# Two transformer blocks in split single precision: residual stream token-major, products 512 columns wide, layers unrolled

## The reference, cut to what matters

```
for l in 2 layers:                                   # block 1
    h = rms_norm(x, ln1)
    proj = h @ w_in                                  # 2866 columns: q, k, v, gates of three mixers
    mixed = [nsa(...), mla(...), retention(...)]     # 17 attention heads of 64 or 96, 5 retention heads
    x = x + mixed @ w_out                            # 1024 x 1024
    h = rms_norm(x, ln2)
    x = x + square(relu(h @ w_up)) @ w_down          # 1024 x 4096, 4096 x 1024
x = rms_norm(x, final_gain)
for l in 2 layers:                                   # block 2
    sh1, sc1, g1, sh2, sc2, g2 = split(silu(c) @ w_ada + b_ada, 6)      # w_ada: 1024 x 6144
    h = rms_norm(x, n1) * (1 + sc1) + sh1
    pool, conv, attention of 8 heads, three gates    # from h @ w_in
    merged = sum of three gated products
    x = x + g1 * (merged @ w_out)
    h = rms_norm(x, n2) * (1 + sc2) + sh2
    x = x + g2 * ((silu(h @ w_gate) * (h @ w_up)) @ w_down)             # 2816 inner features
```

## Time and profile before

| | |
|---|---|
| median of 3 runs | 1811.67 us (1810.47 to 1813.94) |
| the profiled execution: time, span of its trace | 1813.12 us, 1811.3 us |
| PE, DVE, ACT, POOL busy, share of the span | 91%, 63%, 48%, 10% |
| mean granted TensorE clock | 0.907 |
| split products on PE | some 10,400, three for each pair of a weight block and an activation chunk |
| read from memory | 293.67 MB, 163 GB/s over the span |

### The profile page before, as it was taken

How to read it: one execution, slowest core, us unless ns; L and a number is a source line. 1 busy time by engine, 2 the same in 40 slices (tenths; PEclk the granted TensorE clock), 3 DMA queues, 4 the chain that set the end, 5 groups by cost and what they waited for, 6 DMA issues and landing times.

```text
span 1811.3 us, 32196 instructions
## 1 busy us (share of the span) xinstructions
PE 1642.5 (91%) x11986; PEld 1556.2 (86%) x11986; DVE 1142.6 (63%) x1867; ACT 862.2 (48%) x1450; POOL 175.8 (10%) x108
## 2 busy tenths in 40 slices
PE   2998978899799887989979999799997999889999
PEld 2995778899799677979968998799997999879999
DVE  4746868964574686896447755656645864666653
ACT  4443456653443345665337553444444754344442
POOL 0001411300000230230000302100000200300000
PEclk7987589999897658999989999999998999889999
DMA  5432554765343245475523433335553344335552
GB/s 210 164 116 117 185 187 175 299 224 187 111 171 117 104 175 200 183 292 212 184 93 120 183 141 140 139 140 180 179 186 110 140 149 157 138 111 178 180 186 92
DMA packets 41344, 296.89 MB, mean 164 GB/s; under 512 B 4576, under 2 KB 4576, under 8 KB 5600
## 3 DMA queue, kind: packets, MB, share of 16 engines
q1 hardware_dynamic: 40752, 293.57, 44.9%
q10 hardware_dynamic: 432, 1.17, 0.2%
HBM read 293.67 MB, written 1.05 MB: 163 GB/s over the span
## 4 chain that ended last, share of the span: by engine, by line
PE 73%; DVE 13%; issue 7%; ACT 4%; POOL 1%; DMA 1%; DVEq 0%; ACTq 0%; POOLq 0%; SPq 0%
PE acc L708 20%; PE acc L709 20%; PE acc L710 20%; DVE wL L1398 3%; DVE ring L1385 1%; PE acc L852 1%; PE ps_s L784 1%; PE acc L763 1%; PE ps_t L791 1%; PE ps_s L783 1%; ACT wH L1131 1%; DVE hL L1407 1%; PE acc L768 1%; DMA nv<-pos 1%; PE acc L933 1%
## 5 line engine op out<-in xcount | busy, mean ns | idle before, releaser
L708 PE MATMUL acc<-hH,wH 128*128 128x256 f32 x2368 | 700.2, 296 | 91.8 <-DVE hL L1407 72.2
L1398 DVE TENSOR_TENSOR wL<-ring,wH 128x1024 fp32r<-128x1024 f32 x444 | 546.7, 1241 | 300.7 <-ACT wH L1131 299.8
L709 PE MATMUL acc<-hL,wH 128*128 128x256 f32 x2368 | 681.1, 288 | 0.0
L710 PE MATMUL acc<-hH,wL 128*128 128x256 f32 x2368 | 680.5, 287 | 0.0
L1131 ACT ACTIVATE wH<-ring 128x1024 fp32r<-128x1024 f32 x444 | 464.2, 1050 | 229.7 <-PE acc L710 213.4
L708 PEld LDWEIGHTS acc<-hH,wH 128*128 128x128 f32 x2368 | 464.1, 196 | 113.2 <-DVE hL L1407 83.8
L709 PEld LDWEIGHTS acc<-hL,wH 128*128 128x128 f32 x2368 | 466.6, 197 | 2.4 <-issue 1.9
L710 PEld LDWEIGHTS acc<-hH,wL 128*128 128x128 f32 x2368 | 465.8, 197 | 0.0
L708 PE MATMUL acc<-aH,wH 128*128 128x256 f32 x864 | 244.5, 283 | 0.0
L709 PE MATMUL acc<-aL,wH 128*128 128x256 f32 x864 | 244.5, 283 | 0.0
L710 PE MATMUL acc<-aH,wL 128*128 128x256 f32 x864 | 244.5, 283 | 0.0
(11 more groups left out here) (278 smaller groups left out, 2006.1 us busy)
## 6 DMA issues: line engine op xcount, KB each, us to landing
ring<-stream SPq DMA_DIRECT2D x276, 1024.0 KB, 4.8
cst<-consts SPq DMA_DIRECT2D x1, 1669.0 KB, 10.8
x<-xin SPq DMA_DIRECT2D x1, 1024.0 KB, 5.7
out<-x SPq DMA_DIRECT2D x4, 256.0 KB, 4.4
onc<-once ACTq DMA_DIRECT2D x1, 516.0 KB, 10.6
v1all<-vec ACTq DMA_DIRECT2D x1, 371.0 KB, 5.9
v2all<-vec SPq DMA_DIRECT2D x1, 330.0 KB, 11.5
nv<-pos ACTq DMA_DIRECT2D x1, 256.0 KB, 11.7
```

The costliest lines, as they stand in the source:

```text
L708: pe.matmul(out, w[0], y[0], start=first, stop=False)
L709: pe.matmul(out, w[0], y[1], start=False, stop=False)
L710: return pe.matmul(out, w[1], y[0], start=False, stop=last)
L1398: TTN(wL[:, u % SPLIT, :], ring[:, t % RING, half * UNIT:(half + 1) * UNIT], wH[:, u % SPLIT, :].bitcast(F32), ALU.subtract).then_inc(lo_r ...
```

## The change

- `x` is token-major: 2 x 128 tokens on the partitions, 1024 features along the free axis. It is transposed in at the start and out at the end, on PE.
- The down, out (`wo`), value (`v`) and token-major (`tm`) products take the activations as the stationary operand and 512 weight columns as the moving one (`wide_units`, `wo_unit`): for a unit 12 products of 512 columns in place of 24 of 256. Two banks, one for each half of the tokens, are filled together.
- A wide unit takes 128 columns of weights from each of four half tiles. The ring has eight slots of half a tile. Groups of four halves lie in four aligned slots (`align`); `gathered` and `placed` view them for the split.
- Norms: the sum of squares comes from ACT's square with a sum along the free axis (`square`), the root is taken of 128 x 2 elements, DVE scales x into `z` (`normalize`), PE transposes z, ACT makes the high part with the gain (`gained`, `shifted_h`), DVE the low part (`lows`). The first two units after a norm are computed together (`project_both`).
- The gates g1 and g2 of block 2 and the final gain are needed along the free axis now: `diagonals` and two products with ones for each half make rows of them.
- Modulation is computed on DVE alone, a half tile after a unit. No tile of it lies in attention: 2 are among the projections, 10 in up, 12 in down.
- In up, ACT does relu, square and the copy to aH; DVE only the low part.
- The rotary angles are computed after the first four units are fed. The feed of the first four out units stands at step 6 of attention. In block 2 the first out units are interleaved with the mix (`MIX_ORDER`).
- The four hardware loops are gone: the layers are written out.

```diff
-RING = 4
+SLOTS = 8
...
+class Stream:
+    def half(self, kind, j, h, align=1):
+        t = self.tiles.index((kind, j))
+        self.load((kind, j, h), [(t, h * UNIT, UNIT, 0)], align)
+        return (kind, j, h)
+    def unit(self, keys, part, n, name):
+        self.units.append((keys, part, n, name))
+        if self.waiting:
+            self.ada_after[len(self.units) - 1] = [self.waiting.pop(0)]
+    def ada(self, j):
+        for h in range(2):
+            self.waiting.append(self.half("ada", j, h))
+    def wide(self, keys, n, parts, names):
+        for q in range(parts):
+            self.unit(keys, q, n, names[q])
...
+def stream1():
...
+    for u in range(F1 // 2):
+        s.plain("up", u, 0, f"up{2 * u}")
+        s.plain("up", u, 1, f"up{2 * u + 1}")
+        if u % 3 != 2 and u < 15:
+            s.ada(j)
+            j += 1
+    for h in range(2):
+        names = unit_names("dn", h, F1 // 2) + [f"dn{h}1"]
+        for g in range(4):
+            kh, hh = g // 2, g % 2
+            keys = [s.half("down", 2 * n + kh, hh, 4 if n % 4 == 0 else 1) for n in range(4 * h, 4 * h + 4)]
+            s.wide(keys, P, 4, names[4 * g:4 * g + 4])
+            for _ in range(2):
+                if j < N_ADA:
+                    s.ada(j)
+                    j += 1
...
+MIX_ORDER = ["A0", "A1", "A2", "A3", "wo0.0", "A4", "A5", "wo0.1", "A6", "A7", "wo0.2", "wo0.t1"]
...
+def lay_out():
+    loads, at, seq = [], {}, 0
+    latest, landed = [None] * SLOTS, [0] * SLOTS
+    for i, (_, s, _, base) in enumerate(LAYER_LIST):
+        for key, pieces, align in s.loads:
+            seq += -seq % align
+            slot = seq % SLOTS
+            seq += 1
...
+            def wait_free(load):
+                turns, _, L, _ = LAYER_LIST[load.layer]
+                kind, j, h = load.key
+                if kind == "ada":
+                    sp.wait_ge(ada_dve, L * (2 * N_ADA) + 2 * j + h + 1)
+                elif kind in WHOLE_USER:
+                    sp.wait_ge(acc_full, turns.full(WHOLE_USER[kind], L))
+                else:
+                    sp.wait_ge(lo_ready, load.last_unit + 1)
...
+            for load in ALL_LOADS[SLOTS:]:
+                if load.before is not None:
+                    wait_free(load.before)
+                fetch(load)
...
+            def wide_units(names, units, y, n, between=None):
+                outs = [open_acc(name) for name in names]
+                for k in range(units):
+                    wh, wl = [v.rearrange("p (c n) -> p c n", n=512) for v in next_unit()]
+                    for t in range(TT):
+                        for c in range(2):
+                            hh, hl = y(2 * k + c, t)
+                            last = split_product(outs[t][:, 0:n], (hh, hl), (wh[:, c, 0:n], wl[:, c, 0:n]),
+                                                 k == 0 and c == 0, k == units - 1 and c == 1)
+                        if k == units - 1 or t == TT - 1:
+                            last.then_inc(acc_full, 1)
...
             def feed(count):
-                tn, L = fed["tn"], fed["L"]
...
+                    if not unit.part:
+                        for load in unit.loads:
+                            act.wait_ge(got[load.slot], load.landed)
                     if u >= SPLIT:
+                        act.wait_ge(acc_full, ALL_UNITS[u - SPLIT].release)
+                    act.activation(placed(wH, unit, u), gathered(ring, unit), ACT.Copy).then_inc(hi_ready, 1)
...
-                    act.activation(aH[:, n, :], r4[n % 4], ACT.Square).then_inc(aH_ready, 1)
+                    act.activation(tmp4[n % 4], r4[n % 4], ACT.Square).then_inc(up_squared, 1)
+                    act.wait_ge(up_squared, L * F1 + (n + 1))
+                    act.activation(aH[:, n, :], tmp4[n % 4], ACT.Copy).then_inc(aH_ready, 1)
...
+            def feed(count):
+                for u in range(fed["next"], min(fed["base"] + count, len(ALL_UNITS))):
+                    unit = ALL_UNITS[u]
+                    dve.wait_ge(hi_ready, u + 1)
+                    TTN(placed(wL, unit, u), gathered(ring, unit), placed(wH, unit, u).bitcast(F32), ALU.subtract)\
+                        .then_inc(lo_ready, 1)
+                    fed["next"] = u + 1
+                    for key in LAYER_LIST[unit.layer][1].ada_after.get(unit.local, ()):
+                        ada(unit.layer, key)
...
+            def normalize(k, dst=None, row=None):
+                dve.wait_ge(ss_ready, 4 * (k + 1))
+                link(TTN(stat[:, 2, :], sums[:, 0, :], sums[:, 1, :], ALU.add))
+                TSC(stat[:, 0, :], stat[:, 2, :], 1.0 / D, EPS, ALU.mult, ALU.add).then_inc(var_ready, 1)
+                dve.wait_ge(y_ready, roots(k))
+                link(TTN(stat[:, 2, :], stat[:, 1, :], stat[:, 1, :], ALU.mult))
+                link(STT(stat[:, 2, :], stat[:, 0, :], -0.5, stat[:, 2, :], ALU.mult, ALU.mult))
+                link(STT(stat[:, 3, :], stat[:, 2, :], 1.5, stat[:, 1, :], ALU.add, ALU.mult))
+                for h in range(2):
+                    for t in range(TT):
+                        at = slice(512 * h, 512 * h + 512)
+                        if row is None:
+                            TSC(z[:, t, at], x[:, t, at], stat[:, 3, t:t + 1], None, ALU.mult).then_inc(z_ready, 1)
...
-                TTN(products, products, cb2, ALU.mult).then_inc(ada_pool, 1)
```

More of the change, by code:

```diff
@@ L113, in split_units, with __init__, load, plain @@
[L113 to L120 removed]
+class Stream:
+    def __init__(self, tiles):
+        self.tiles = tiles
+        self.loads, self.units, self.ada_after = [], [], {}
+        self.waiting = []
+    def load(self, key, pieces, align=1):
+        self.loads.append((key, pieces, align))
+    def half(self, kind, j, h, align=1):
[6 more added lines that the diff above has]
+            self.ada_after[len(self.units) - 1] = [self.waiting.pop(0)]
+    def plain(self, kind, j, h, name):
+        self.unit([self.half(kind, j, h)], None, None, name)
+    def whole(self, kind):
+        for h in range(2):
+            self.half(kind, 0, h, 2 if h == 0 else 1)
+    def ada(self, j):
[4 more added lines that the diff above has]
+            self.unit(keys, q, n, names[q])
+    def end(self):
+        self.ada_after.setdefault(len(self.units) - 1, []).extend(self.waiting)
+        self.waiting = []
+        return self
@@ new lines, in by_columns, with out_half, blocks_at @@
+def by_columns(s, kind, js, names):
+    for h in range(2):
+        keys = [s.half(kind, j, h, 2 if j == js[0] else 1) for j in js]
+        s.wide(keys, 256, 2, names[2 * h:2 * h + 2])
+def out_half(s, h):
+    return [s.half("wout", n // 2, n % 2, 4 if n % 4 == 0 else 1) for n in range(4 * h, 4 * h + 4)]
+def blocks_at(m, count):
+    first = min(count, 16 - m % 16)
+    out = [(m // 16, (m % 16) * P, first * P, 0)]
+    return out + ([(m // 16 + 1, 0, (count - first) * P, first * P)] if first < count else [])
@@ L641, in rest @@
-            def rest(tiles, turns, units, lo_base, layer, first):
-                for t in range(RING, len(tiles)):
-                    wait_free(tiles, turns, units, lo_base, layer, t - RING)
-                    load(t % RING, first + t)
-            def ahead(tiles, turns, units, lo_base, layer, first):
-                n = len(tiles)
-                for t in range(n - RING, n):
-                    wait_free(tiles, turns, units, lo_base, layer, t)
-                    load(t % RING, first + n + t % RING)
@@ L1028, in _, with mix @@
                 pe.wait_ge(yc_ready, L * 2 + 2)
[L1029 removed]
+                def mix(n):
                     wh, wl = blocks(next_unit())
@@ L1119, in feed, with square @@
-            def feed(count):
-                tn, L = fed["tn"], fed["L"]
-                for u in range(fed["next"], min(count, len(fed["units"]))):
-                    t, half, _ = fed["units"][u]
-                    slot = t % RING
-                    if half == 0:
-                        n = len([v for v in range(len(fed["tiles"])) if v % RING == slot])
-                        act.wait_ge(got[slot], L * (16 * n) + 16 * (fed["visits"][slot] + t // RING + 1))
+            def square(junk, h, t):
+                act.activation(junk[:, 2 * h + t, :], x[:, t, 512 * h:512 * h + 512], ACT.Square,
+                               accum_out=sums[:, h, t:t + 1]).then_inc(ss_ready, 1)
@@ L1285, in _ @@
                     feed(units_before(i + 1) + SPLIT)
+                    if i in ROWS_AT:
+                        for g in range(2):
+                            take(A2, f"row{ROWS_AT[i]}{g}", L, rows[ROWS_AT[i]][:, 512 * g:512 * g + 512], n=512)
                     if i in SQUARES_AT:
@@ L1777, in _ @@
+            normalize(2 * LAYERS, row=gain_row)
+            end_layer()
+            for L in range(LAYERS):
+                fed["base"] = UNIT_BASE[LAYERS + L]
                 nc.vector.memset(up_[:, :, 0:16], 0.0)
```

1009 lines of the change are left out of this document (586 added, 423 removed).

## The result

The changed kernel took 1911.99 us (median of 4 runs, 1908.34 to 1916.78), the one before 1812.12 beside it: 1.055 times as long, 95% interval 1.052 to 1.058. I had forecast 1792, range 1745 to 1828, and slower with a chance of 0.20. What I took for a small gain is a loss of 100 us.

A forecast was written before the change was run, and what follows sets the result against it. The prediction took TensorE's (PE's) stream to set the end, with 73% of the chain. Gains of 129 us less losses of 110 took the span from 1811.3 to a forecast of 1792 us, range 1745 to 1828.

The forecast's parts named there:

- The ring stall: In down of block 1, weight groups and modulation halves leave no second buffer, so PE stops: 103 us lost in all.
- Up: Modulation on VectorE alone, without slow DVE instructions beside POOL's, saves 9.5 us a layer in up, 19 us.
- The first product: At the start, first product near 22 us instead of 40.05, fifth near 45.5 instead of 55.5; 8.5 us gained.
- Layer to layer in block 1: Boundary after down of block 1: PE's wait falls from 13 us to about 7.8, a gain of 4.6.
- the landing term of the ring: In down of block 1, five half tiles land 8.3 us after release, making a group's cycle 18.9 us.
- Rival C: Ring cycle longer than 21 us, through dearer strided feeds or a queue behind SP: 1816 to 1835 us, chance 0.10.
- the mix: In block 2, out units between mix products partly fill PE's idle time: 2.5 us a layer, 5 gained.
- Block 2's projections: Projection segment of block 2 grows by 2.2 us over both layers.
- Wide products: Products of 512 columns take 0.216 us, replacing two of 256 at 0.240 together; 51 us gained with token-major.
- Boundaries: Shorter waits around norms gain 29.5 us, including final norm 9, out to up 0.5 twice, block 2 layer to layer 7.3.
- attention: Block 1's attention loses its 14 modulation tiles a layer: 8 us a layer, 16 gained, between 4 and 13.
- the likeliest case: Ring stall against the other gains, ending at 1760 to 1808 us; chance 0.66.

The follow-up runs named there:

- run 2: Changed kernel without the 12 modulation tiles in down of block 1 (loads, product and sum left out, half of the modulation zero): 1777.80 us, 0.983 times before.
- run 12: Changed kernel, groups and layout kept, all modulation computed but moved out of down of block 1 into up and the projections: 1843.38 us, 1.020 times before.
- run 1: Changed kernel with block 1's down weights in memory as used, one wide unit in one half tile: 1843.61 us, 1.019 times before.
- run 7: Changed kernel with its own weight layout, all mix chunks first and then the out units: 1874.02 us, 1.037 times before.
- run 3: Changed kernel with block 2's out weights in memory as used, one wide unit in one half tile: 1894.70 us, 1.047 times before.
- run 6: Run 5's kernel with all eight mix chunks of block 2 ahead of the first half's out units: 1723.14 us, 0.953 times before.
- run 8: Run 6's kernel with VectorE splitting the units after block 2's value units ahead of the second rotary step: 1718.68 us, 0.951 times before.
- run 9: Run 8's kernel with block 2's rotary step ahead of the refinement in the two steps that have both: 1699.08 us, 0.939 times before.
- run 5: Changed kernel with all wide-product weights laid out as used, and units alternating with modulation halves in down of block 1: 1760.73 us, 0.974 times before.

## Why the prediction was wrong

**What held.** The ring stall was the right mechanism: its place, its five long stops a layer (8.3 to 10.9 us for 8 to 9), the 10.5 us of DVE's order, and that groups alone don't cause it (runs 2 and 12). Groups aren't the whole of it either: without them, in run 1, a cycle of 17.1 us is left. Up gained 20.9 for 19. The first product came at 25.2 (forecast 22), the fifth at 48.4 (45). Layer to layer in block 1 PE waits 8.5 us (7.8).

**The step that failed first: the landing term of the ring.** "The next group lands 2.1 + 6.2 = 8.3 later" measured 11.1, the cycle 22.3 and 22.9 instead of 18.9. I had priced an empty queue, 2.1 us and then five transfers at 426 GB/s, the best short stretch in the earlier trace rows. The rate itself came nearly true from the second landing on; what failed is the start. The bunch is issued one load after another behind a half that is still landing, and its first half takes 3.9 to 6.6 us instead of 3.3, so that over the 11.2 us from release to landing the queue moved 258 GB/s at a share of 0.75. Five passages a layer at 3.4 to 4.0 us make 17 to 20, both layers 37 of the 41 us of that row. Rival C (a cycle over 21 us, 0.10) is what happened here, and not through dearer feeds, since the split from four slots takes 1.235 us on average (1.241 before). Its other reason, "a queue behind SP", fits; how much of the 2.8 us is the 1.50 us issue, how much the half under way and how much a slower first transfer, no run separates. (My own working has three slips that move nothing: the terms of a layer add to 49.2, not 49.5, those of a boundary to 7.6, not 7.8, and a group's 2.1 MB at 426 GB/s and 2.1 us to 7.0, not 7.4.)

**The largest: the mix, in a step I gave 5 us of gain.** "Out units between the mix products fill part" saw that each waits for a merged chunk but took the wait to be shorter than the two chunks between. Merging is a path over DVE, POOL, ACT and DVE and outlasted them by 4.2 to 5.3 us each time. And the rule for the ring that I applied to down I did not apply here: the second out group needs the slots of the first. Of the 171.8 us of both segments the order alone gives back 38.0 (run 7), the layout alone 13.6 (run 3), both 51.5 (run 6): two causes, and they add up. With both gone the two segments are 120.4, against 113.3 in the forecast, and most of that rest is the boundary, whose gain stands in the next row.

**Block 2's projections,** where I had 2 us of cost for two layers and 17.7 came: I counted products and rows, but not that a wide unit opens two banks at once and that one value step instead of two moves every rotation and refinement against the units around them. Three stops of 3 us, two for a bank and one for a split; runs 8 and 9 take them away, and 11.6 us of the segment go, since the slow products after each stop go too.

**Wide products: 0.227, not 0.216.** I took the 0.013 that a product costs beyond its columns for a weight load that a longer product would cover. It stays: 512 columns at 2.4 GHz are 0.213, and 0.227 - 0.213 is again 0.013. The row that I trusted, the full-precision product at 512, doesn't show that addition, and it doesn't carry over to this data type. A wide product saves one such addition, 0.013 for each of 1776, 23 us where I had 43; 402 columns took 0.188 (forecast 0.170), and the projections with token-major gained 3.4 a layer where no stop is in them (second layer), for 4.2. The Trainium skill, "TensorE: Matmul & The Clock Gate", section "Back-to-back issue gap", has an isolated gap of 216 ns for this width; the measurement is 227, and its sustained 131 ns appears in none of the gapless stretches here.

**Boundaries.** Layer to layer in block 1 gained 4.5 for 4.6, the final norm went from 22.2 to 16.2 (forecast 15.6). Out to up lost 0.7 a layer where I had 0.5 of gain, again with slow products behind it that count to up. Layer to layer in block 2 went from 13.4 to 10.1 us, 3.3 for 7.3. That is a part of the 13.1 that down of block 2 missed; 5.8 are the dearer wide products, and some 3 are the evacuation and transposes at the very end, which I had put in the last row.

**Too low a gain** stood at attention, 27.9 for 16; no run separates its parts. The 10.2 of gate and up, where I had nothing, are the boundary's, as said below the table.

Together, in the order of the table: 8.0 - 11.9 + 4.6 - 1.9 + 41.2 + 15.5 + 58.5 - 10.2 + 13.1 - 2.4 = 114.5, the span of 1906.5 less the 1792 of the forecast. Chances: I gave the ring a correct place and then kept the likeliest case narrow, though three unmeasured waits (landings, merging, banks) all pointed upwards.

**The better version.** Run 9 takes 1699.08, 6.1% less than before and 11% less than the change as it was made: taken together, the wide products, the norms and the modulation on VectorE are worth their cost once loads, mix and rotations stand in another order. What each of them is worth alone wasn't run. Its page:

```profile
span 1696.0 us, 25582 instructions
...
PE 1569.8 (93%) x10054; PEld 1424.3 (84%) x10054; DVE 1111.0 (66%) x1857; ACT 860.0 (51%) x1483; POOL 59.0 (3%) x60
...
PE 85%; DVE 7%; ACT 5%; issue 2%; POOL 1%; DMA 0%; ACTq 0%; DVEq 0%
```

## What to carry to other kernels

When a change makes several buffers come free together, write down for every stage which load waits for which release, and what stands behind that load in the same queue; a ring that holds two groups is single-buffered as soon as anything else passes through it. Lay weights out in the order in which they are used: here that cost nothing on the chip and removed the group. Then spread the loads evenly, because separate slots alone brought back only half of the stall. Work put between other work to fill a wait helps only if its own inputs are older than the longest path that makes them, and an in-order engine must empty a bank before it waits for anything else.

## What the runs showed of the hardware

- The queue's rate isn't one number. At nearly full share half tiles in packets of 4096 B moved 337 GB/s over 87 us (run 5) and 404 over the 3.5 us from 381.5 to 385.0 (changed kernel), against 426 over 8 us in the earlier trace rows, there in packets of 8192 B. In the same bunch, from 379.5 to 381.0, a share of 0.96 moved only 235. So a full share doesn't mean a full rate; why wasn't tried.
- A half tile behind an idle queue landed 3.8 us after its issue (369.60 to 373.36), the first of a bunch 3.9 to 6.6, the following ones mostly 1.25 to 1.3 apart.
- A split product in sequence costs its columns and 0.013 us at 256 as at 512 columns, at full clock. That is no rule for other widths: 402 columns took 0.188, which is 0.020 over their 0.168. At half clock 512 columns took 0.427, their columns alone.
- After a stop (3.3 us ahead of 368.49) wide products run at half clock for 3.5 us, 0.43 apart; a group of down takes 12.4 us or more behind a stop and 10.7 without. In a cycle that the ring sets this costs nothing; behind the stops of block 2 it does: the three stops of 3 us there go with 11.6 us of the segment (runs 8 and 9).
